# A new order of eleven projection slots, and a later place for the layer norm's transposes, in the mixer of a decoder layer

## What is computed

```python
def layer_norm(x, g, b):
    x32 = x.astype(jnp.float32)
    mu = jnp.mean(x32, axis=-1, keepdims=True)
    xc = x32 - mu
    y = xc * lax.rsqrt(jnp.mean(xc * xc, axis=-1, keepdims=True) + EPS)
    return (y * g.astype(jnp.float32) + b.astype(jnp.float32)).astype(x.dtype)
...
def conformer_conv(a, gate, w_dw, b_dw, ln_g, ln_b):
    v = a * jax.nn.sigmoid(gate)
    v = causal_dwconv(v, w_dw) + b_dw
    v = layer_norm(v, ln_g, ln_b)
    return jax.nn.silu(v)

def short_gated_conv(bg, cg, xv, w):
    return bg * causal_dwconv(cg * xv, w)
...
        h = rms_norm(x, mix_pre_norm[l])
        z = h @ w_in[l]
        zp, za, zg, zb, zc, zx = jnp.split(z, split_at, axis=-1)
        ya = pool_mixer(zp, pool_maps[l], pool_scale[l])
        yb = conformer_conv(za, zg, conf_dw_w[l], conf_dw_b[l], conf_ln_g[l], conf_ln_b[l])
        yc = short_gated_conv(zb, zc, zx, sconv_w[l])
        y = jnp.concatenate([ya, yb, yc], axis=-1) @ w_out[l]
        x = x + rms_norm(y, mix_post_norm[l])
```

## Time and profile before

| | us |
|---|---|
| median of 3 runs | 2698.38 |
| lowest, highest | 2696.05, 2699.09 |
| the profiled execution | 2691.14 |
| its span in the trace | 2689.3 |
| TensorE matmul busy | 2549.9 (95%) |
| VectorE busy | 1579.4 (59%) |
| ScalarE busy | 966.0 (36%) |
| GpSimd busy | 982.5 (37%) |

### The profile page before, as it was taken

How to read it: one execution, slowest core, us unless ns; L and a number is a source line. 1 busy time by engine, 2 the same in 40 slices (tenths; PEclk the granted TensorE clock), 3 DMA queues, 4 the chain that set the end, 5 groups by cost and what they waited for, 6 DMA issues and landing times.

```text
span 2689.3 us, 33390 instructions
## 1 busy us (share of the span) xinstructions
PE 2549.9 (95%) x11713; PEld 2114.1 (79%) x11713; DVE 1579.4 (59%) x2446; ACT 966.0 (36%) x1565; POOL 982.5 (37%) x394
## 2 busy tenths in 40 slices
PE   7869899999998998999999999999999999999997
PEld 6657788878877787777888878888878888778886
DVE  4898888777736547447626456346276264562462
ACT  5323322232235444453433433333434334233332
POOL 6451400000023443333444444534444444345342
PEclk9989999999999999999999999999999999999999
DMA  8785585665834524435333244332353332443331
GB/s 243 232 317 196 196 302 177 240 251 209 307 125 172 195 79 179 166 95 185 95 110 94 81 142 147 109 94 95 87 189 96 107 94 84 133 128 107 91 94 63
DMA packets 318417, 410.59 MB, mean 153 GB/s; under 512 B 12584, under 2 KB 235069, under 8 KB 305469
## 3 DMA queue, kind: packets, MB, share of 16 engines
q1 hardware_dynamic: 309709, 396.62, 44.3%
q10 hardware_dynamic: 8560, 12.06, 1.3%
HBM read 343.62 MB, written 65.01 MB: 152 GB/s over the span
## 4 chain that ended last, share of the span: by engine, by line
PE 77%; DVE 14%; issue 5%; ACT 2%; DMA 1%; POOL 1%; DVEq 0%; ACTq 0%; SPq 0%; POOLq 0%
PE colb L1411 15%; PE colb L1413 15%; PE colb L1412 15%; PE accb L1411 10%; PE accb L1413 10%; PE accb L1412 10%; DVE arena L1147 3%; PE colb L1448 2%; DVE xh L1087 1%; DVE arena L1310 1%; DVE xh L1014 1%; DVE small L1008 1%; DVE small L1301 1%; ACT junk L656 1%; POOL pair L604 1%
## 5 line engine op out<-in xcount | busy, mean ns | idle before, releaser
L604 POOL TENSOR_TENSOR pair<-raw,pair 128x1024 fp32r<-128x1024 f32 x387 | 981.6, 2551 | 1676.2 <-ACT pair L635 1676.0
L1411 PE MATMUL colb<-hT,pair 128*128 128x512 f32 x1952 | 765.8, 392 | 18.8 <-issue 15.5
L1413 PE MATMUL colb<-hT,pair 128*128 128x512 f32 x1952 | 762.2, 390 | 0.0
L1412 PE MATMUL colb<-hT,pair 128*128 128x512 f32 x1952 | 762.0, 390 | 0.0
L635 ACT ACTIVATE pair<-raw 128x1024 fp32r<-128x1024 f32 x387 | 406.0, 1054 | 541.9 <-PE accb L1413 314.5
L1354 DVE TENSOR_SCALAR arena<-arena,par 128x512 f32<-128x512 f32 x176 | 246.1, 1438 | 375.5 <-ACT arena L938 375.0
L1411 PE MATMUL accb<-pair,act 128*128 128x512 f32 x1120 | 440.2, 393 | 18.7 <-issue 6.2
L1411 PEld LDWEIGHTS colb<-hT,pair 128*128 128x128 f32 x1952 | 368.3, 189 | 102.8 <-issue 27.1
L1413 PE MATMUL accb<-pair,act 128*128 128x512 f32 x1120 | 437.3, 390 | 0.0
L1412 PE MATMUL accb<-pair,act 128*128 128x512 f32 x1120 | 436.9, 390 | 0.0
L1413 PEld LDWEIGHTS colb<-hT,pair 128*128 128x128 f32 x1952 | 367.9, 188 | 77.5
(11 more groups left out here) (150 smaller groups left out, 2395.2 us busy)
## 6 DMA issues: line engine op xcount, KB each, us to landing
raw<-in_ffn_w_up SPq DMA_DIRECT2D x176, 512.0 KB, 3.8
pair<-kept SPq DMA_DIRECT2D x75, 1024.0 KB, 4.9
raw<-in_ffn_w_down SPq DMA_DIRECT2D x176, 256.0 KB, 2.9
kept<-pair SPq DMA_DIRECT2D x25, 1024.0 KB, 5.1
raw<-att_a SPq DMA_DIRECT2D x64, 256.0 KB, 3.0
raw<-att_b SPq DMA_DIRECT2D x64, 256.0 KB, 5.9
raw<-in_w_in SPq DMA_DIRECT2D x17, 512.0 KB, 6.6
xh<-in_x SPq DMA_DIRECT2D x4, 2048.0 KB, 14.2
```

The lines of the kernel that those rows point to most:

```text
L604: nc.gpsimd.tensor_tensor(pair[:, b, 1, :], raw[:, r, :], pair[:, b, 0, :].bitcast(F32), ALU.subtract).then_inc(lo_done, 1)
L1411: nc.tensor.matmul(dst, sh, mh, start=first, stop=False)
L1412: nc.tensor.matmul(dst, sh, ml, start=False, stop=False)
L1413: return nc.tensor.matmul(dst, sl, mh, start=False, stop=last)
```

## The change

A list `R_ORDER` gives a new order to the slots r. The columns c of all three short-convolution chunks (2, 5, 8) now come first, then x and b of chunk 0 (3, 4), of chunk 1 (6, 7), and of chunk 2 (9, 10). On TensorE, slots 5, 8, 3, 4 and 6 stand ahead of the layer norm's transposes where 3, 4 and 5 stood, and 7 and 9 stand behind them where 6 to 9 stood. On ScalarE the calls of `rest` follow the new order, and `round_y(5)` now comes behind `rest` of six slots, of which the last is `rest(7)`, in eleventh place. VectorE's code is not changed; the banks that it reads are numbered anew.

```diff
+    R_ORDER = [0, 1, 2, 5, 8, 3, 4, 6, 7, 9, 10]
-    MIX_HEAD = [("r", 0), ("q", 0), ("r", 1), ("q", 1)] + [("r", i) for i in range(2, 10)] +\
+    MIX_HEAD = [("r", 0), ("q", 0), ("r", 1), ("q", 1)] + [("r", i) for i in R_ORDER[2:10]] +\
                [("o", 0), ("o", 1), ("r", 10), ("out", 0, 0), ("out", 0, 1)]
...
     MIX_ITEMS = [("r", 0)] + WQ_ITEMS[0] + [("r", 1)] + WQ_ITEMS[1] +\
-                [("r", i) for i in range(2, RSLOTS)] + [("row", k) for k in range(KD)] + [("crow", j) for j in range(NC_)]
+                [("r", i) for i in R_ORDER[2:]] + [("row", k) for k in range(KD)] + [("crow", j) for j in range(NC_)]
...
                 a_rows(1)
-                for i in range(3, 6):
+                for i in R_ORDER[3:9]:
                     rest(i)
-                rest(6)
                 round_y(5)
-                rest(7)
-                rest(8)
+                rest(9)
                 round_y(0)
-                rest(9)
                 round_y(1)
                 next_squares(p, t)
...
                 a_rows(3)
-                for i in range(3, 6):
+                for i in R_ORDER[3:8]:
                     rest(i)
...
-                for i in range(6, 10):
+                for i in R_ORDER[8:10]:
                     rest(i)
                 b_rows(0)
```

## The result

| | before | after |
|---|---|---|
| median, us | 2697.22 (4 runs) | 2722.41 (4 runs) |
| lowest, highest | 2694.32, 2699.09 | 2721.80, 2725.60 |
| profiled execution | 2691.14 | 2721.80 |
| its span | 2689.3 | 2720.0 |

A forecast was written before the change was run, and what follows sets the result against it. VectorE was taken to bound the first tile, TensorE the later ones, with ScalarE's late o1 deciding the cost. 0 + 3 x 7.7 = 23.1 us on the 2698.38 us median gave 2721.5 us, range 2712 to 2730.

The forecast's parts named there:

- What would show it: Signs expected in the profile after: moved waits on TensorE and VectorE, ScalarE's rounding order, later tiles about 170 us.
- First tile, 0 within -2.5 to +3: First mixer tile: filling TensorE's 20.0 us wait gains nothing, as VectorE bounds that stretch; cost 0, -2.5 to +3 us.
- the bound named: First tile's lower limit: GpSimd's subtractions of o0 and o1 may leave VectorE's run, worth 2.5 us.
- Tiles two to four, 7.7 us each: Later tiles: chunk 5, rounded behind o1's conversion, delays pooling, squares and out(0,1); 7.7 us later in each of three.
- The cause, ScalarE's order with a late o1: Tiles two to four: ScalarE's rounding of chunk 5 stands behind o1's awaited conversion; this decides the 7.7 us per tile.
- Nearly free: Tiles two to four: transposes 10.9 us later are mostly absorbed by VectorE's idle time; TensorE feels 0.2 to 2 us.
- the pooling's 10.3 us: Tiles two to four: VectorE's time for chunk 5's low part and both pooling chunks, 10.3 us, taken from the old profile.
- The new slot order, 0: Rest of the order (banks, early columns c, b2 and x2 sooner): only fills buffers earlier, hidden by TensorE's slots; 0.
- Rival 1: First tile's 20 us wait was on the path, so the two slots gain 10.9 us: 2687.5 us; 4%.
- Rival 2: The o1 weights are there in time, so later tiles cost 0.2 to 2 us each: 2699 to 2704 us; 5%.
- Rival 3: It costs more through slower o1 loads and added restarts, at most 11 us on top: 2727, up to 2732; 10%.
- Rival 4: Half of it comes: VectorE or ScalarE shorten a step, 8 to 14 us remain: 2706 to 2712 us; 6%.

The follow-up runs named there:

- e4: Kernel before, with the new order of slots, ScalarE and TensorE in the first mixer tile only: 2690.91 us, ratio 0.9989.
- e11: Changed kernel, with GpSimd's subtractions for o0 and o1 cut to 16 columns in tiles two to four: 2713.99 us, ratio 1.0080.
- e1: Kernel before, with only ScalarE's new order (chunk 5 rounded behind the conversions of o0 and o1): 2732.51 us, ratio 1.0152.
- e2: Changed kernel, with ScalarE rounding chunk 5 ahead of the conversions of o0 and o1: 2704.55 us, ratio 1.0044.
- e9: Changed kernel, with chunk 5 rounded ahead of o0 and o1 and the tile's row load issued behind o1's: 2708.44 us, ratio 1.0055.
- e5: Changed kernel, with the load of the tile's rows issued two places later, behind o1's: 2705.46 us, ratio 1.0054.
- e6: Kernel before, with the load of the tile's rows issued two places later, behind o1's: 2685.57 us, ratio 0.9976.
- e3: Changed kernel, with the layer norm's transposes back behind three slots and ScalarE's order as changed: 2721.69 us, ratio 1.0110.
- e12: Kernel before, with GpSimd's subtractions for o0 and o1 cut to 16 columns in tiles two to four: 2683.46 us, ratio 0.9972.
- e8: Kernel before, with the new order in the first mixer tile only and the row load issued two places later: 2684.91 us, ratio 0.9965.
- e7: Kernel before, with 4 of the 31 convolution taps left out in the preparation phase, 8 us less VectorE work: 2689.29 us, ratio 0.9986.
- e10: Changed kernel, with chunk 5 rounded early, rows loaded later and GpSimd's o0 and o1 subtractions cut to 16 columns: 2692.57 us, ratio 1.0002.

## Why the prediction was right

**Slower by 23: right, but that it came so close is partly luck.** The forecast was 2721.5 us and the median came to 2722.41. The forecast laid 23.1 us on a median of before that stands high among its sets; against the four others, 2691.5 to 2694.7, the change costs 28 to 31 us, as in the traces. What would show it was there point by point: a first wait of about 9 us (11.3), a new one before the first w_out slot (6.25 rather than 10), no rounding between the last copy of c and the conversion of o0, VectorE's idle time ahead of chunk 5's low part (7.41 us), 5 to 6 us of standing before out(0,0) (5.87, 7.42 and 5.62). VectorE's first run ended 1.5 us sooner than the 237 that was expected.

**First tile, 0 within -2.5 to +3: right in size, through another subtraction than the bound named.** e4 measured -3.0 (-5.4 to -0.5), the trace -1.5. In VectorE's run before, three groups were stretched by GpSimd's subtractions (L1112 2.03, one L1182 pair 2.45 and one L1178 pair 3.72 instead of 0.68, 0.37 and 1.53, together 5.6 us), after it two (L1148 2.31 instead of 0.17, an L1203 pair 3.57 instead of 1.54, 4.2 us). The subtractions of o0 and o1, which the bound let leave the run, stayed in it both times, 3.4 us before and 4.2 after. The one that stopped costing is that of slot 10, here before and after:

```profile
213.94 2.39 POOL L604 TENSOR_TENSOR pair<-raw,pair 128x1024 fp32r<-128x1024 f32 x1 [3.70 <-ACT pair L635]
213.93 3.72 DVE L1178 SCALAR_TENSOR_TENSOR arena<-arena,inv_full 64x512 f32<-64x512 f32 x2
...
204.73 2.40 POOL L605 TENSOR_TENSOR pair<-raw,pair 128x1024 fp32r<-128x1024 f32 x1 [6.40 <-ACT pair L636]
204.78 2.44 DVE L1238 TENSOR_SCALAR arena<-accb,small 128x384 f32<-128x384 f32 x4
```

After, it falls on the normalised rows, which VectorE reads from PSUM; they take 2.44 us, with no GpSimd work beside them in the second tile 2.43.

**Tiles two to four, 7.7 us each: mechanism right, the size too small in the trace.** The profiled execution shows 10.5, 9.0 and 10.3. For the second tile the terms are: o1 0.7 us later, measured from the tile's start; the low part of chunk 5 2.42 instead of 0.68 us, because it falls on GpSimd's subtraction of o1, 1.7 us that I had allowed for in the first tile and forgotten here; and the way from out(0,0) to out(0,1) 9.35 instead of 8.7 us. e11, without that subtraction, is 4.6 us faster than after by the ratios, as expected of it. The medians differ by 25.2 us and so lie nearer to the forecast than these terms do; that is the high median of before, as said above, and not a better account.

**The cause, ScalarE's order with a late o1: right, but it is not all.** e1 makes the loss alone, e2 takes ScalarE's order away and with it 14 of 26 us, and e9 against e5 shows that the order costs nothing once o1 is early. The forecast gave this cause all 7.7 us of a tile; the other 12 us of the loss stay without it.

**"Nearly free", 0.2 to 2 us for late transposes: wrong.** It was hidden behind the larger cause, so it did not hurt the sum, but e2 shows 4 to 5 us a tile with the late o1, and e9 against e6 some 7 with an early one. The step that failed took the pooling's 10.3 us from a place where GpSimd was idle; in e2 the same steps took 14.4 (382.51 to 396.91), since one L1171 under each subtraction took 2.79 and 2.72 us instead of 0.71. It also compared the pooling chunks' end with the wrong event, VectorE's low part of chunk 0 at 393.16. ScalarE's squares stand behind the rounding of chunk 1, which needs the second pooling chunk; they started at 393.55 before and could not start before 396.2 by my own times. That makes 2.65 us of lateness on the path, where I let TensorE feel 0.2 to 2.

**"The new slot order, 0": right only beside the rest.** e1 and e3 differ in it alone, 41 against 30 us, so it saves 11 us where ScalarE is late. In the later tiles the freer bank of slot 10 is the row that shows it; 4.5 of the 11 lie in the first tile.

**The rivals.** Rival 1 (the 20 us wait pays 10.9 us) is refuted by e4. Rival 2 (o1 in time) was made true in e5, and the change then still cost 14.5 us instead of 1 to 6, or 21 against e6, by the same error as above. Rival 3 (it costs more) came in part: o1 was later, by 0.7 us instead of 1.5, and the traces show 30.7 us. Rival 4 (half of it) did not come.

## What to carry to other kernels

A long wait is worth only what its releaser leaves over: ask when the engine that ends it is next waited for, and fill it if that engine has slack. In a list of steps written by hand, a step that others need must not stand behind a step that waits for a transfer, and a transfer must not stand behind one that waits for a store: the second alone cost this kernel 6.5 us (e6), the first 14 us in the new slot order (e2) and 41 in the old one (e1). Before a run of two-input VectorE work is moved, look at what GpSimd does at the new place.

## What the runs showed of the hardware

One GpSimd subtraction of 128 x 1024 elements takes two very different times beside the same run of 24 VectorE operations. Before and in e12, GpSimd and VectorE at the start of the second tile:

```profile
300.17 15.34 POOL L604 TENSOR_TENSOR pair<-raw,pair 128x1024 fp32r<-128x1024 f32 x1 [4.64 <-ACT pair L635]
```

```profile
297.32 15.99 DVE L1147 SCALAR_TENSOR_TENSOR arena<-arena,par 128x512 f32<-128x512 f32 x24
```

```profile
299.70 2.76 POOL L605 TENSOR_TENSOR pair<-raw,pair 128x1024 fp32r<-128x1024 f32 x1 [4.67 <-ACT pair L636]
```

```profile
296.82 18.12 DVE L1148 SCALAR_TENSOR_TENSOR arena<-arena,par 128x512 f32<-128x512 f32 x24
```

Either GpSimd gets through and the run is 2.1 us longer, or the subtraction takes 15.3 us and ends only 2.2 us after the run, and TensorE waits 5.87 us for it. Nothing is changed near this place: the traces of before, after, e4, e6, e8 and e9 have the long one, those of e1, e2, e3, e5, e7, e11 and e12 the short one, and e10 one of 13.7 us. Between before and e12 the way from the first tile's mark to the second tile's transposes is 120.8 against 118.7 us, so 2 us of any difference between two traces may be this alone. What is held for a subtraction's length need not be large. In the first tile before, VectorE and GpSimd:

```profile
224.97 2.41 DVE L1008 SCALAR_TENSOR_TENSOR small<-small 128x4 f32<-128x4 f32 x1
...
224.96 4.93 POOL L604 TENSOR_TENSOR pair<-raw,pair 128x1024 fp32r<-128x1024 f32 x2 [8.63 <-ACT pair L635]
```

An operation on 128x4 elements took 2.41 us instead of 0.16, much as one on 128x512 took 2.42 instead of 0.68 (L1110 in the kernel after), while the four that read PSUM (L1238, shown above) were not held at all. So VectorE's many tiny steps are as exposed as its large ones. The Trainium skill, "GPSIMD Engine Reference", Key points, says that GpSimd contends with VectorE instructions that have two SBUF inputs or run in a 2-port mode. The rows with two inputs agree. A 128x30 copy with one input was held too, from 0.17 to 2.31 us; whether it ran in such a mode no run here shows.

A restart of TensorE after nearly the same idle time came at either clock: 12 matmuls took 3.00 us after 2.38 us (before, second tile) and 4.52 us after 2.42 us (after, the same place), the latter in a window with a mean granted clock of 0.63. In both kernels the engine had worked without a stop since before the transposes (366.27, 376.28). The Trainium skill, "TensorE: Matmul & The Clock Gate", What's actually happening, says that the default state is throttled and activity releases it; the windows shown above agree, but no run here tells which of two like pauses loses the clock.
